# Three gate chunks of branch A as seven block products, in a decoder step on one core

## The reference, cut to what matters

```python
proj = xn @ w_in     # -> a_b, a_c, a_x, b_val, b_glu, q, gate_logits
ya, new_a = causal_dwconv(buf_a, a_c * a_x, conv_a_w)     # width 3
ya = (a_b * ya) @ w_out_a
ub = b_val * sigmoid(b_glu)
yb, new_b = causal_dwconv(buf_b, ub, conv_b_w)            # width 31
yb = silu(layernorm(yb + conv_b_bias)) @ w_out_b
yx = attention(q, mem_k, mem_v) @ w_out_x
g = sigmoid(gate_logits + b_gate)                         # 3 x 1024
merged = g[:, :, 0] * ya + g[:, :, 1] * yb + g[:, :, 2] * yx
h = x + merged @ w_o
h = h + (silu(hn @ w_ff_gate) * (hn @ w_ff_up)) @ w_ff_down
```

## Time and profile before

| | us |
|---|---|
| median of 3 runs | 1065.08 |
| the profiled execution | 1064.31 |
| its span in the trace | 1062.4 |
| branch B, chunks 4 to 7 (seven products) | 112.19 to 152.45 |
| branch X | 321.7 to 413.8 |
| chunks `C_BA`, state rows | 413.8 to 460.6 |
| branch A | 460.63 to 553.19 |
| mean and gate chunks of branch B | 553.19 to 601.0 |

### The profile page before, as it was taken

How to read it: one execution, slowest core, us unless ns; L and a number is a source line. 1 busy time by engine, 2 the same in 40 slices (tenths; PEclk the granted TensorE clock), 3 DMA queues, 4 the chain that set the end, 5 groups by cost and what they waited for, 6 DMA issues and landing times.

```text
span 1062.4 us, 20369 instructions
## 1 busy us (share of the span) xinstructions
PE 1051.5 (99%) x8703; PEld 1044.8 (98%) x8703; DVE 764.7 (72%) x1290; ACT 489.2 (46%) x560; POOL 114.5 (11%) x93
## 2 busy tenths in 40 slices
PE   9999999999999999999999999999999999999997
PEld 8999999999999999999999999999999999999996
DVE  6797888889888775686742855488777557688754
ACT  6745554544334353453446623344455245366432
POOL 4671000002300000000000000000000000000000
PEclk9999999999999999999999999999999999999999
DMA  8958787789787778668876653321687355487512
GB/s 299 293 172 198 170 214 195 221 211 306 234 242 160 198 198 181 176 156 197 199 188 158 172 203 117 98 82 48 158 214 169 118 140 140 126 201 181 158 40 81
DMA packets 155353, 186.19 MB, mean 175 GB/s; under 512 B 4822, under 2 KB 145454, under 8 KB 150262
## 3 DMA queue, kind: packets, MB, share of 16 engines
q1 hardware_dynamic: 121894, 106.64, 32.1%
q0 software_dynamic: 8496, 56.10, 26.6%
q10 hardware_dynamic: 24880, 22.26, 6.8%
HBM read 122.34 MB, written 7.54 MB: 122 GB/s over the span
## 4 chain that ended last, share of the span: by engine, by line
PE 90%; DMA 5%; POOL 1%; ACT 1%; DVE 1%; ACTq 0%; issue 0%; SPq 0%; DVEq 0%; POOLq 0%
PE acc L2436 38%; PE acc L2454 19%; PE acc L2860 11%; PE acc L2812 9%; PE acc L2819 5%; PE acc L2622 3%; DMA w_raw<-in_w_v_dram 2%; POOL w_l L776 1%; PE acc L2630 1%; DMA ws_l<-w_raw 1%; PE acc L2701 1%; PE acc L2408 1%; PE acc L2677 1%; DMA w_raw<-in_w_ff_gate_dram 1%; DMA w_raw<-in_w_ff_up_dram 1%; DMA w_raw<-in_w_k_dram 1%
## 5 line engine op out<-in xcount | busy, mean ns | idle before, releaser
L2436 PE MATMUL acc<-big_h,w_h 128*128 128x260 f32 x1536 | 310.8, 284 | 0.0
L2436 PE MATMUL acc<-big_l,w_h 128*128 128x260 f32 x1536 | 308.5, 282 | 0.0
L2436 PEld LDWEIGHTS acc<-big_h,w_h 128*128 128x128 f32 x1536 | 236.1, 188 | 0.5
L2436 PEld LDWEIGHTS acc<-big_l,w_h 128*128 128x128 f32 x1536 | 236.5, 188 | 0.0
L2454 PE MATMUL acc<-big_h,w_l 128*128 128x260 f32 x1536 | 193.0, 282 | 0.0
L2454 PEld LDWEIGHTS acc<-big_h,w_l 128*128 128x128 f32 x1536 | 188.1, 188 | 0.2 <-DMA w_l<-w_raw 0.2
L1573 DVE SCALAR_TENSOR_TENSOR ubyb<-ubyb,prm 128x512 f32<-128x512 f32 x240 | 180.3, 751 | 7.1
L807 ACT ACTIVATE w_h<-w_raw 128x1024 fp32r<-128x1024 f32 x112 | 112.2, 1052 | 95.3 <-DMA w_raw<-in_w_in_dram 29.5
L2812 PE MATMUL acc<-x_h,ws_h 128*128 128x260 f32 x504 | 125.9, 282 | 0.3 <-ACT cp L1299 0.2
L2812 PE MATMUL acc<-x_l,ws_h 128*128 128x260 f32 x504 | 125.7, 282 | 0.0
L2812 PEld LDWEIGHTS acc<-x_h,ws_h 128*128 128x128 f32 x504 | 94.8, 188 | 0.7 <-ACT cp L1299 0.7
(11 more groups left out here) (335 smaller groups left out, 1537.8 us busy)
## 6 DMA issues: line engine op xcount, KB each, us to landing
w_l<-w_raw POOLq DMA_DIRECT2D x37, 1024.0 KB, 8.1
w_raw<-in_w_in_dram SPq DMA_DIRECT2D x32, 1024.0 KB, 5.6
ws_l<-w_raw POOLq DMA_DIRECT2D x18, 768.0 KB, 6.5
w_raw<-in_w_ff_gate_dram SPq DMA_DIRECT2D x18, 512.0 KB, 5.3
w_raw<-in_w_ff_up_dram SPq DMA_DIRECT2D x18, 512.0 KB, 5.2
k_st<-in_cache_mem_k_dram ACTq DMA_DIRECT2D x8, 1024.0 KB, 9.0
v_st<-in_cache_mem_v_dram ACTq DMA_DIRECT2D x8, 1024.0 KB, 13.6
w_raw<-in_w_v_dram SPq DMA_DIRECT2D x4, 1024.0 KB, 8.5
```

The source lines that it names most:

```text
L2436: last = M.matmul(out[:, b, 0:HALF], w_h[:, slot, k, cols], xs[:, k_at + k, b * HALF:(b + 1) * HALF], start=start and k == 0 and xs is x[0 ...
```

## The change

`SEVENS` takes the place of `GLU_SEVEN` as the list of seven-product chunks: the four of branch B and `C_A + 2`, `C_A + 4`, `C_A + 6`. The helpers take a chunk number now. New activation blocks `ta` are made on DVE in branch X (sums of high and low part of `xn` by quarters, then four turnings), their high parts on ACT and low parts on DVE beside the chunks `C_BA`. The loops of branch A on PE and ACT are written out. `taps` are spread anew. `uao`, from which the state rows are stored, moves to the place of `sg`, and ACT waits for both stores before it writes there; the stores stand behind the split of `C_A + 1`. `ln_sum` gets a place of its own and all of its seven additions stand behind the last steps of the convolution.

```diff
+SEVENS = (*(C_B + j for j in GLU_SEVEN), *range(C_A + 2, C_A + 8, 2))
+def nth(c):
+    return SEVENS.index(c)
...
-    uao = at("uao", [TS + 2, D], f32, o_p2h)
+    ta = [at(f"ta_{n}", [P, 4, PAIRS, HALF], f32r, o) for n, o in (("h", o_p2h), ("l", o_p2l))]
+    ta_f = at("ta_f", [P, 4, PAIRS * HALF], f32, o_p2l)
...
     sg = at("sg", [P, 2, SG], f32, o)
     up_f = at("up_f", [P, 2 * TOK], f32, o)
+    uao = at("uao", [TS + 2, D], f32, o)
...
-                if isinstance(c, int) and c - C_B in GLU_SEVEN:
+                if c in SEVENS:
                     for half, b, landed_ in ((1, 0, w_half), (0, 2, w_loaded)):
...
+            def blocks_hi(c):
+                sums_hi(c, 0)
+                sums_hi(c, 1)
+                nc.scalar.activation(wq_h[:, c % 2, 1:4, :].rearrange("p b n -> p (b n)"),
+                                     raw_f[:, c % 2, 1:4, :].rearrange("p b n -> p (b n)"), ACT.Copy).then_inc(w_hi, 2)
+            def first_copy(c, u, quarter):
+                act.wait_ge(b_prod, 3 * nth(c) + 3)
+                if c % 2 == 0:
+                    act.wait_ge(acc_read, u)
+                nc.scalar.activation(quarter, acc[u % 4][:, 0, 0:HALF], ACT.Copy).then_inc(b_copy, 1)
...
+                if 1 <= n <= 4:
+                    act.wait_ge(t_step, 14)
+                    nc.scalar.activation(ta[0][:, n - 1, :, :].rearrange("p r t -> p (r t)"), ta_f[:, n - 1, :], ACT.Copy) \
+                        .then_inc(t_hi, 1)
-            act.wait_ge(acc_read, T["ctail"] + 1)
-            act.dma_start(conv_a_prompt[0, 0], uao[0:2, :]).then_inc(uao_stored, 16)
-            act.dma_start(conv_a_sample[0, :, 1, :], uao[2:2 + TS, :]).then_inc(uao_stored, 16)
-            gate_stage(T["a"], C_A, R_BG + BR_A, a_sig)
+            for it in range(4):
+                c, u0 = C_A + 2 * it, T["a"] + 4 * it
+                if it:
+                    first_copy(c, u0, quarters(0)[0])
+                split(c + 1, 1, u0 - 1)
+                if it == 0:
+                    act.wait_ge(acc_read, T["ctail"] + 1)
+                    act.dma_start(conv_a_prompt[0, 0], uao[0:2, :]).then_inc(uao_stored, 16)
+                    act.dma_start(conv_a_sample[0, :, 1, :], uao[2:2 + TS, :]).then_inc(uao_stored, 16)
+                    act.wait_ge(uao_stored, 32)
+                elif it < 3:
+                    seven_minus(c + 2, u0 + 1)
+                for j in range(2):
+                    if it == 0:
+                        done(u0 + j)
+                        act.wait_ge(acc_read, u0)
+                        logits = halves(u0 + j)
+                    else:
+                        act.wait_ge(acc_read, u0 + 2)
+                        logits = two(sg[:, j, 2:SG])
+                    nc.scalar.activation(two(sg[:, j, 2:SG]), logits, ACT.Sigmoid, bias=param(2 * it + j, R_BG + BR_A)) \
+                        .then_inc(a_sig, 1)
+                if it == 3:
+                    split(C_GB, 0, u0 + 1)
+                else:
+                    if it == 0:
+                        seven_minus(c + 2, u0 + 1)
+                    blocks_hi(c + 2)
...
+            def quarter_again(n):
+                ks, toks = ((0, early), (1, late), (0, late), (1, early))[n]
+                src = [x[:, ks * PAIRS:(ks + 1) * PAIRS, toks] for x in xn]
+                V.tensor_tensor(ta_f[:, n, :].rearrange("p (r t) -> p r t", t=HALF), f(src[0]), f(src[1]), ALU.add) \
+                    .then_inc(t_step, 1)
+            def turned_again():
+                q1, q2, q3, q4 = (ta_f[:, n, :] for n in range(4))
+                dve.wait_ge(t_step, 10)
+                V.tensor_tensor(q1, q1, q3, ALU.subtract).then_inc(t_step, 1)
...
             for p in range(4):
                 u0 = T["x"] + 4 * p
-                taps(16 if p else 12)
+                if p == 1:
+                    for n in range(4):
+                        quarter_again(n)
+                elif p == 2:
+                    turned_again()
+                taps((12, 14, 14, 16)[p])
...
-                taps(4 if n % 2 else 3)
+                if n >= 4:
+                    m = n - 4
+                    dve.wait_ge(t_hi, 4 + m + 1)
+                    V.tensor_tensor(ta[1][:, m, :, :].rearrange("p r t -> p (r t)"), ta_f[:, m, :],
+                                    f(ta[0][:, m, :, :]).rearrange("p r t -> p (r t)"), ALU.subtract).then_inc(t_lo, 1)
+                taps(3 if n >= 4 else 5)
             ba_lo_part(KT - 1)
             done(T["ctail"])
+            dve.wait_ge(acc_read, T["x"] + 16)
             V.tensor_copy(uao[:, :].rearrange("p (b c) -> p b c", b=2), acc[T["ctail"] % 4][0:TS + 2, :, :]) \
...
+            def sum_tiles():
+                dve.wait_ge(so_lo, NH)
+                dve.wait_ge(cs_step, KT)
+                dve.wait_ge(cv_step, KT * K_B)
+                for k in range(1, KT):
                     V.tensor_tensor(ln_sum[:, :], ubyb[:, k, 0:TOK], ubyb[:, 0, 0:TOK] if k == 1 else ln_sum[:, :],
                                     ALU.add).then_inc(ln_step, 1)
...
             for it in range(4):
-                u0 = T["a"] + 4 * it
+                c, u0 = C_A + 2 * it, T["a"] + 4 * it
+                taps((6, 3, 4, 4)[it])
+                if it:
+                    first_sums(c, u0, quarters(0))
+                    taps((6, 6, KT * CV - made)[it - 1])
+                    last_sums(c, u0, quarters(0))
                 if it < 3:
-                    taps(((14, 5), (14, 4), (14, 4))[it][0])
+                    if it == 0:
+                        dve.wait_ge(ba_lo, KT)
+                    seven_sums(c + 2, 0, u0 + 1)
+                    seven_sums(c + 2, 1)
+                    sums_low(c + 2, 0)
+                    sums_low(c + 2, 1)
+                    taps((5, 5, 5)[it])
                 else:
-                    sum_first_tiles()
-                    dve.wait_ge(cs_step, KT)
-                    dve.wait_ge(cv_step, KT * K_B)
-                    V.tensor_tensor(ln_sum[:, :], ubyb[:, KT - 1, 0:TOK], ln_sum[:, :], ALU.add).then_inc(ln_step, 1)
+                    sum_tiles()
                 dve.wait_ge(a_sig, 2 * it + 2)
...
-                        .then_inc(acc_read, 1 if j else 3)
-                    if it < 3 and j == 0:
-                        taps(((14, 5), (14, 4), (14, 4))[it][1])
+                        .then_inc(acc_read, 3 if it == 0 and j == 0 else 1)
...
-            pairs(T["a"], C_A, (xn, br), (ba_lo, KT))
+            for j in range(8):
+                c, u = C_A + j, T["a"] + 2 * j
+                if j == 1:
+                    pe.wait_ge(ba_lo, KT)
+                if j == 2:
+                    pe.wait_ge(t_lo, 8)
+                if c in SEVENS:
+                    seven_products(c, u, ta)
+                else:
+                    chunk(c, j % 2, u, u, (xn, br)[j % 2])
```

## The result

The changed kernel takes 1068.24 us (median of 11 runs, 1067.29 to 1069.47), the kernel before on the same chip 1065.08: a ratio of 1.0029, interval 1.0020 to 1.0037. It is slower by 3.2 us where 3.8 were to be gained. The profiled execution took 1067.66 us.

The account below looks back on a forecast made before the run. TensorE, busy 99%, was taken as the bound. 4.3 us from matmuls, less 0.44 at A2, plus 0.14, less 0.1 to 0.2 for `ln_sum` and 0.1 for DMA meetings, gave 3.8: 1061.3 us, full range 1060.3 to 1065.2.

Parts of the forecast that it names:

- TensorE, -4.3 us for three chunks: Branch A's gate chunks A2, A4, A6: seven products take 10.07 us in place of 11.51, 1.44 us less each.
- `ta` work and convolution steps hidden: Branch X and chunks BA0 to BA3: additions, +3.4 us on VectorE, fit in 4.59 us of idle; turnings and copies hidden too.
- A2 at 484.35, 0.44 us given back: Start of A2: VectorE's work ends at 484.2, so TensorE goes on at 484.35 where it did at 483.91.
- The store's landing: State-row store before A2's sigmoids: lands 2.6 us after issue, at 472.4, no loss; at 4.0 us, 1.1 us lost.
- The formula named beside it: State-row store: a transfer takes about 2.0 us plus bytes over 436 GB/s, 2.1 us here; the sum would be the same.
- The store rival: State-row store ahead of A2: lands in 4.0 us rather than 2.6, A2 at 485.5, kernel 1062.4 us; chance 0.08.
- VectorE's slip and `ln_sum`: A2 to A7: VectorE's room falls from 1.5 to 0.5 us without stopping TensorE; `ln_sum` ready 0.1 us after A7 ends.
- become the bound: Rival in branch A: VectorE becomes the bound, price about 1.7 us, kernel 1063.0 us; chance 0.16.
- Low parts by DMA: A3, A5, A7 and branch B's first gate chunk: accumulating DMA takes 6.9 to 8 us, no stall, 1 to 2 us of room.
- Behind it everything shifts as it is: From the mean to the end: everything hangs on TensorE and shifts unchanged, keeping the gain of 3.8 us.

Follow-up runs that it names:

- e1: Changed kernel, with ScalarE making A2's negated copy and high parts ahead of its wait for the two stores: 1062.48 us, ratio 0.9974 to the kernel before.
- e10: Changed kernel, GpSimd holding A1's accumulating DMA until the state rows stand in SBUF, 26 filling products written as 4: 1061.53 us, ratio 0.9967 to the kernel before.
- e2: Changed kernel, with the two state-row stores issued between A1's high copies and negated copy, before A1's accumulating DMA: 1062.33 us, ratio 0.9977 to the kernel before.
- e6: Changed kernel with A1's accumulating DMA over half of the chunk (512 KB), the rest left out, for timing alone: 1064.82 us, one run.
- e12: Kernel before with branch A's loops on TensorE and ScalarE written out and the 26 filling products written as 4: 1065.58 us, ratio 1.0006 to the kernel before.
- e3: Kernel before with branch A's loops on TensorE and ScalarE written out, nothing else: 1065.32 us, ratio 1.0002 to the kernel before.
- e11: e10 with branch X's TensorE loop written as two chunks in the loop and four written out: 1060.86 us, ratio 0.9962 to the kernel before.
- e10_again: The same kernel as e10, run again on the chip of e11: 1060.66 us, ratio 0.9959 to the kernel before.
- e4: e2 with branch X's TensorE loop written as two chunks in the loop and four written out: 1061.85 us, ratio 0.9973 to the kernel before.
- e8: e2 with the 26 filling products at the start written as 4 wide ones: 1061.62 us, ratio 0.9966 to the kernel before.

## Why the prediction was wrong

- **TensorE, -4.3 us for three chunks: right.** A4 lasts 10.06 us, A5 11.49. With the stall out of the way (e1, e10) the stage is 4.29 us shorter (93.44 to 89.15); 3.9 were forecast.
- **`ta` work and convolution steps hidden: right.** Up to A2, TensorE waits for none of it in the changed kernel's profile.
- **A2 at 484.35, 0.44 us given back: near, but with a wait put down to the wrong cause.** In e1 and e10 TensorE waits 0.4 us for the `merged` add, and A2's first product starts 24.41 us behind the flips; in the kernel before it does so at 24.14 (483.74), and the forecast amounts to 24.75. So 0.3 us were given back there. The 0.27 us at 479.80, which the prediction gave to this wait, belong to A1's low part: its accumulating DMA landed at 479.76, and the page of the kernel before has the weight loads (PEld) of the low products idle for that DMA, once, for 0.2 us:

```profile
L2454 PEld LDWEIGHTS acc<-big_h,w_l 128*128 128x128 f32 x1536 | 188.1, 188 | 0.2 <-DMA w_l<-w_raw 0.2
```

  In the changed kernel that DMA is issued 3.4 us earlier and nothing waits for it. One small loss went and another grew, and nearly the whole 4.3 us were kept.
- **The store's landing: the step that failed.** The prediction took 2.6 us from a row of a store of the same size, and 4.0 as its upper end from a larger one. The size was the wrong thing to match. These stores take 2.2 us or less with no accumulating DMA ahead (e2), and the second one, of 32 KB, is issued 1.4 us behind one of 1024 KB: it landed with it, 6.6 us after its issue (e6 and e2 show that it follows that DMA, e1 that TensorE's stall hangs on it). Both durations stood in the earlier trace rows; the prediction put the DMA's 6.9 us into its account of the low parts and not into the store's. It also named the chain behind the wait rightly (sigmoids, negated copy, high parts, VectorE's low parts), and that chain turned 4.0 us of late landing into 3.8 of stall. The formula named beside it (2.1 us) is given by the Trainium skill, page "DMA: Bandwidth & Descriptors", for the path of transfers issued from GpSimd, and ScalarE issues this store; it has no term for what is under way ahead.
- **The clock: not in the sum.** The store rival priced the stall and not what comes behind it: 1.5 us more in A2 for products at 1.2 GHz after a gap of 3.8. After a gap of 1.2 us (e6) the clock stayed. So the store rival was the right mechanism at about a fifth of its size: it was priced at 1.1 us (1062.4), and taking the stall away was worth 5.2 (1067.63 to 1062.48).
- **VectorE's slip and `ln_sum`: right.** No wait for the first sums in A2, A4 or A6; the mean follows A7 at once. VectorE did not become the bound.
- **Low parts by DMA: right.** No wait for them after A2.
- **"Behind it everything shifts as it is": wrong by 1.6 to 1.7 us.** The tail grew by the waits for `cp` (2.1 us in place of 0.2 to 0.3), behind two loads that were used about 1 us later. In part this goes with where TensorE's program is fetched: it is 36 matmuls shorter ahead of the tail and has its loops written out, and a packet fell into those loads. e12 against e3 has a tail 1.4 us longer without any of the change, e11 against e10_again one 0.8 us shorter with all of it. Each pair differs in its program's place and in what that shifts.

The 3.8 us of the forecast are within what the kernels with the change and without the stall reached: 2.3 to 4.2 us under the kernel before (e1, e2, e4, e8, e10, e11). What stands open: that the packets alone make the difference in the tail. Moving the program also shifts things at other places (the start, A1's low part), and the whole time never moved by more than 1.3 us for it; in e4 the waits for `cp` stayed at 1.5 us with both loads used by 9.9, and in the two pairs above (e12, e11) the time did not follow the tail. Why a packet 7 us behind the issue goes with a later load than one at 1 us was not tried. What length of gap brings the clock down was not tried either.

## What to carry to other kernels

A small transfer whose landing someone waits for can cost what is left of a large one issued just before it (here 6.6 us in place of 2). Take its price from that one, and issue it first, hold the large one back a moment, or put the work that does not need the landing ahead of the wait. A stall of several microseconds on TensorE must be priced with the slower matmuls behind it (here 3.8 us and 1.5 more). When a change adds or drops instructions of an engine, stages that it doesn't touch may move by a microsecond; compare several placements before a difference of 0.1% is called the change's.

## What the hardware did that was not expected

- A store of 8 KB and one of 32 KB, issued 1.1 and 1.4 us behind an accumulating DMA: both had landed 6.6 us after the second one's issue behind 1024 KB, 4.0 behind 512 KB, each time 0.2 us behind that DMA; in 2.2 us or less with no such DMA ahead, in 1.8 us when the second store was issued 0.2 us ahead of it.
- A packet of TensorE's program (16 KB, about 1 us of one DMA engine of 16) inside a load's flight goes with a later landing: two halves of 512 KB beside an accumulating DMA were used at 9.7 us with the packet's start ahead of the issue or 8.7 us and more behind it (mean of 13), at 10.2 with it 0.0 to 5.4 us behind (4), at 10.8 with it 6.9 to 8.5 us behind (13). That the packet is the cause is argued, not isolated.
- The granted clock fell to 0.50 behind a gap of 3.8 us and stayed at 1.00 behind one of 1.2.
